# Spreading the last sixteen projection steps of two attention heads over their large query tiles

## The reference

```python
def block(args):
    qi, ci, s0 = args
    logits = jnp.einsum('bqhd,bkhd->bhqk', qi, k, preferred_element_type=jnp.float32) * scale
    logits = logits + (ci[..., :, None] - cum_k[:, :, None, :])
    qpos = s0 + jnp.arange(Q_BLOCK)
    mask = kpos[None, :] <= qpos[:, None]
    logits = jnp.where(mask[None, None], logits, -jnp.inf)
    p = jax.nn.softmax(logits, axis=-1)
    return jnp.einsum('bhqk,bkhd->bqhd', p.astype(v.dtype), v)
```

## Time and profile before

| | |
|---|---|
| median of 3 runs | 2994.4 us (2992.97 to 2999.1) |
| profiled execution, its time | 3002.76 us |
| its span | 3001.0 us |
| mean granted TensorE clock | 0.989 |
| PE busy | 2912.7 us, 97% of the span |
| DVE busy | 1492.5 us, 50% |
| ACT busy | 923.7 us, 31% |
| POOL busy | 1108.4 us, 37% |

### The profile page before, as it was taken

One profiled execution on the slowest core, in us unless ns is written; L12 is line 12 of the kernel. 1 busy time (PEld: TensorE's weight loads), 2 busy tenths in 40 slices (PEclk: granted clock), 3 DMA queues, 4 the chain that ended last, 5 costly groups with the idle time before them and its releaser, 6 DMA issues. The chain is left out here.

```text
span 3001.0 us, 37184 instructions
## 1 busy us (share of the span) xinstructions
PE 2912.7 (97%) x14772; PEld 2432.3 (81%) x14772; DVE 1492.5 (50%) x2202; ACT 923.7 (31%) x1628; POOL 1108.4 (37%) x585
## 2 busy tenths in 40 slices
PE   7999999999999999999999999999899999999997
PEld 3877778888888888888888887888788888888886
DVE  5842227887734413123134444545626666664645
ACT  5122226665113101011010111420325656563401
POOL 1332351111596434444343444334332332332341
PEclk9999999999999999999999999999899999999998
DMA  6534574331443111111111111111152222221111
GB/s 246 188 126 143 182 242 133 91 87 40 174 149 113 57 49 43 49 50 50 50 50 50 49 64 56 44 49 43 36 176 71 71 68 71 73 72 47 43 50 63
DMA packets 123821, 263.00 MB, mean 88 GB/s; under 512 B 48476, under 2 KB 74540, under 8 KB 119424
## 3 DMA queue, kind: packets, MB, share of 16 engines
q1 hardware_dynamic: 123648, 260.57, 26.2%
HBM read 215.97 MB, written 46.06 MB: 87 GB/s over the span
## 5 line engine op out<-in xcount | busy, mean ns | idle before, releaser
L881 POOL TENSOR_TENSOR whi<-raw,onesf 128x1024 fp32r<-128x1024 f32 x187 | 360.8, 1929 | 1293.1 <-PE ps L439 1188.1
L437 PE MATMUL ps<-Hb_hi,whi 128*128 128x512 f32 x1424 | 568.6, 399 | 10.3 <-DVE Y L2847 5.9
L439 PE MATMUL ps<-Hb_hi,wlo 128*128 128x512 f32 x1424 | 555.7, 390 | 0.0
L438 PE MATMUL ps<-Hb_lo,whi 128*128 128x512 f32 x1424 | 554.8, 390 | 0.0
L883 POOL TENSOR_TENSOR wlo<-raw,whi 128x1024 fp32r<-128x1024 f32 x187 | 500.2, 2675 | 14.7
L437 PEld LDWEIGHTS ps<-Hb_hi,whi 128*128 128x128 f32 x1424 | 267.7, 188 | 64.4 <-issue 8.5
L439 PEld LDWEIGHTS ps<-Hb_hi,wlo 128*128 128x128 f32 x1424 | 267.3, 188 | 57.1
L438 PEld LDWEIGHTS ps<-Hb_lo,whi 128*128 128x128 f32 x1424 | 268.1, 188 | 48.8
L1907 ACT ACTIVATE tmp<-ps 64x256 f32<-64x256 f32 (+3 forms) x112 | 61.7, 551 | 535.8 <-PE ps L439 465.3
L1907 ACT ACTIVATE tmp<-tmp,mx 128x1280 f32<-128x1280 f32 (+2 forms) x192 | 187.1, 974 | 80.7 <-DVE mx L3125 50.6
L437 PE MATMUL ps<-Uhi,whi 128*128 128x512 f32 x512 | 199.2, 389 | 0.0
(11 more groups left out here) (468 smaller groups left out, 5846.1 us busy)
## 6 DMA issues: line engine op xcount, KB each, us to landing
raw<-in_w SPq DMA_DIRECT2D x197, 512.0 KB, 3.5
adas<-in_ada SPq DMA_DIRECT2D x16, 1024.0 KB, 4.9
raw<-in_w SPq DMA_DIRECT2D x44, 256.0 KB, 3.8
adaE<-in_ada SPq DMA_DIRECT2D x4, 2048.0 KB, 23.0
gate_d<-gst SPq DMA_DIRECT2D x16, 512.0 KB, 2.8
v_d<-VS SPq DMA_DIRECT2D x2, 4096.0 KB, 14.2
ncB<-cum_d SPq DMA_DIRECT2D x16, 512.0 KB, 3.5
Vx<-v_d SPq DMA_DIRECT2D x16, 512.0 KB, 3.8
```

The lines of the kernel that those rows point to most:

```text
L437: nc.tensor.matmul(o, wh, xh, start=start, stop=False)
L438: nc.tensor.matmul(o, wh, xl, start=False, stop=False)
L439: return nc.tensor.matmul(o, wl, xh, start=False, stop=stop)
L881: nc.gpsimd.tensor_tensor(whi[b][:, 0:w], raw[b][:, 0:w], onesf[:, 0:1].to_broadcast([P, w]), ALU.mult).then_inc(S("split_hi"), 1)
```

## The change

Three things change, for heads 14 and 15 alone. The table `FILL_LAST` takes steps from rounds 2 to 5 and puts them into rounds 6, 7 and 8. ACT evicts the second half behind its last `flip_hi` of the head, not at tile 5. DVE evicts it behind its last `flip_lo` of the head, not at tiles 5 to 7.

```diff
 FILL = (4, 4, 4, 3, 2, 1, 2, 1, 2, 1)
-FILL_LAST = (3, 3, 3, 3, 2, 2, 0, 0, 0, 0)
+FILL_LAST = (3, 3, 2, 2, 1, 1, 1, 1, 2, 0)
...
# ACT's program
-                        if qt in (2, 5) and mine:
+                        if qt in (2, 5) and mine and not (qt == 5 and h >= FOX - 2):
                             project(*mine[qt // 4])
                     flip_hi(h, 7)
+                    if h >= FOX - 2:
+                        project(*mine[1])
                 other_half(FOX - 1, 3)
...
# DVE's program
                         if qt == 2 and mine:
                             project(*mine[0])
-                        if qt >= 5 and mine:
+                        if qt >= 5 and mine and h < FOX - 2:
                             kind, which, half = mine[1]
                             if kind == "kq":
                                 keys_queries(which, half, qt - 5)
...
                     for x in range(2):
                         flip_lo(h, 7, x)
+                    if h >= FOX - 2:
+                        project(*mine[1])
                 add(FOX - 1, 3)
```

## The result

| | before | changed |
|---|---|---|
| median, same comparison | 2997.16 us (12 runs, 2992.97 to 3002.98) | 3005.49 us (12 runs, 3001.99 to 3010.96) |
| profiled execution, its time | 3002.76 us | 3005.51 us |
| its span | 3001.0 us | 3003.7 us |

The changed kernel takes 1.0024 times as long, with an interval of 1.0015 to 1.0033: it is slower, by 8.3 us in the medians. The forecast was +5.2 us and 2999.6 us; the interval, 4.5 to 9.9 us, holds the difference, but the time lies outside the range of 2993.0 to 3003.5 us.

A forecast was written before the change was run, and what follows sets the result against it. PE sets the pace, with 4.82 us of pauses in heads 14 and 15. Rounds gave -2.27 us, 5.73 us more waiting at the border made +3.46, with the clock +5.2: 2999.6 us, range 2993.0 to 3003.5.

The forecast's parts named there:

- The likeliest case: Border of heads 14 and 15: late decay row, then 1.2 GHz for 2 to 5.4 us; +5.2 us, chance 0.47.
- the last line of the sum: Whole kernel: the +5.2 us put on a median of 2994.4 us, giving 2999.6 us, 0.17% more.
- part 3: Queue behind head 14's step 16: split, panel load and decay row slip; flips(15, 0) 4.48 us later, PE waits 6.5 us.
- Parts 1 and 2: Rounds of heads 14, 15: late waits removed, -2.56 and -1.50 us; thinner early rounds cost +0.83, +0.48, +0.48 us.
- 4.37 to the load: Chain behind step 16: SP issues the panel load 4.37 us after POOL begins splitting panel 25.
- The eviction ... lies wholly under this wait: Ahead of head 15's first tile: three ACT and three DVE instructions hidden under PE's 6.5 us wait for the row.
- rival A: Border of heads: decay row not held up, DVE's order decides; -0.9 us, 2993.5 us; chance 0.08.
- Part 4: Behind the pause at flips(15, 0): clock at 1.2 GHz for 3.6 us, 1.7 us lost, bounds 0 and 3.3.
- Rival B: Behind the pause: row late but clock stays at 2.4 GHz; +3.5 us, 2997.9 us; chance 0.12.
- rival C: Behind the pause: clock stays at 1.2 GHz for 7.0 us, 3.3 us lost; 6.8 us slower, 3001.2 us; chance 0.28.
- Rival D: Memory heads: keys and values late behind the split after head 15's step 16; about 1 us; chance 0.03.
- Rival E: Heads 14 and 15: every wait won, 4.82 us; 2989.6 us; chance 0.02.

The follow-up runs named there:

- e1: Changed kernel with head 15's decay row issued ahead of the panel load in SP's queue; stretch 67.80 us, ratio 1.0008 to the kernel before.
- e5: Kernel before, with its own table, but head 14's and 15's second half evicted behind the head's last flips; stretch 65.72 us, no ratio.
- e7: Changed kernel with 36 unused matmuls on PE ahead of flips(15, 0) to fill the pause; stretch 71.99 us, no ratio.
- e2: Changed kernel with only the table altered, so step 16 comes ahead of flips(14, 6); stretch 69.84 us, ratio 1.0007 to the kernel before.
- e10: As e6, with another table: three steps in round 2, two in round 4, none in round 5; stretch 63.88 us, ratio 0.9991 to before.
- e3: Changed kernel with 24 unused matmuls on PE ahead of flips(15, 0); stretch 73.22 us, ratio 1.0022 to the kernel before.
- e6: Changed kernel, decay row ahead of panel load, head 14's second half evicted behind head 15's first row_max and exps; stretch 63.51 us, 0.9986 to before.

## Why the prediction went wrong, point by point

**The likeliest case was the one that happened; the time was not in the range.** The forecast had the mechanism, its place and its sign, and a sum of +5.2 us. The three traces of the changed kernel give 5.5, 6.3 and 6.5 us more than before, the medians 8.3.

**The step that failed first** is the last line of the sum, "on it the change gives 2994.4 + 5.2 = 2999.6 us". The median of three runs that it stands on lay low: over the twelve runs of the comparison that tried the forecast it was 2997.16 us, in later comparisons on two chips 2998.78 and 3000.25 us, and single executions took 3000.23, 3001.13 and 3002.76. That is 2.8 us of the 5.9 that were missing, and it decides: with the base at 2997.16 the same range would have ended at 3006.3 us and held the 3005.49. Of the other 3.1 us the traces show 0.9 (6.1 us on average, where +5.2 was forecast), mostly in part 3 below; for 2.2 us they show nothing. The start of head 14 scatters by 7 us, which one trace can't show; the distance of 8.4 us between the profiled execution and the median was the hint. The clock has a part in this scatter, since its low stretches ahead of head 14 differ from trace to trace: by windows of 1 us PE worked at 0.50 for 34 us in the trace of before and for 26 us in e1, whose head 14 begins 7.0 us earlier. At 47% lost that is an estimated 4 of these 7 us.

**Parts 1 and 2, the rounds: right in the main.** The waits of the earlier trace rows went as forecast. `flips(14, 3)` waits 0.72 us (0.83 forecast), `flips(14, 4)` 0.81 (0.48), `flips(15, 4)` 0.57 (0.48), nothing at tile 5 and at `flips(15, 3)`. The rounds had 4.06 us of waits and have 2.10: -1.96 us, where -2.27 was forecast.

**Part 3, the queue: right in kind, mis-sized.** The term is "that is 5.73 us more of waiting". Measured, `flips(15, 0)` waits 7.30, 7.91 and 7.76 us and not 6.5, where it was 0.76: 6.5 to 7.2 us more. The main cause is the step "4.37 to the load": from POOL's start at 2694.45 to SP's load at 2699.56 it took 5.11 us, since the first half of the split ran into DVE's gate multiply and took 2.64 us, not 1.89. The other miss is the landing, 4.3 to 5.0 us in the changed kernel, inside the bounds of 3.5 and 5.0 that I gave, with 4.5 taken. A third, of 0.3 us, is POOL's start, half of it since I hung the chain on the start of `flips(14, 7)`, while POOL waits for the end of step 16's last matmul. The 0.38 us from load to row are exact. From `flips(14, 7)` to `flips(15, 0)` pass 11.05 us; 10.3 was forecast.

**"The eviction ... lies wholly under this wait": true, and it hid a second cause.** In the changed kernel the row is later than the CAST. Without the queue (e1) rival A's case comes about, for which I had -0.9 us; the stretch was 1.3 us longer than before. The forecast priced the eviction by two instructions, "0.68 + 0.69", which holds with POOL idle (e5), and took neither the CAST's collision with POOL's split (0.42 to 1.73 us) nor a fallen clock into account. The causes cover each other: mending the queue alone (e1) gave back 4.9 of 6.1 us and uncovered the rest. The reverse, the changed kernel with only the eviction moved, was not run.

**Part 4, the clock: right in kind, too dear.** 1.7 us forecast, 1.0 to 1.3 measured (rest 62.7 against 61.7 before and 61.4 in e7), since PE worked 3.0 us at 1.2 GHz and not 3.6. Rival B is out, rival C too: its 7.0 us are about what the low level lasted (6.8), but 3.9 us of them lay under the pause and cost nothing. The forecast counted the low level from the end of a pause only. e2, with 5.6 us of work at 1.2 GHz behind a shorter pause, shows what that leaves out.

**Rival D did not occur.** The fourth load for the memory heads went out at 2735.50 us, 4.8 us ahead of their first scores, and PE had no wait for them; the one wait there, 0.82 us for `Y`, is in both kernels. It was missing from the forecast's list, so "All this is 4.82 us, and no more can be won" does not hold: PE's waits in the stretch were 5.64 us. **Rival E** is out.

**What stays open.** The sum of the three terms agrees with the traces (-1.96 + 6.54 + 1.0 = 5.6, and 5.5 read off), but the medians differ by 8.3 and 7.0 us. Both intervals hold 5.5 to 6.5 us; whether the changed kernel loses more than the stretch shows in the executions without a trace stays open. One thing beyond it is shown: in e1, e2 and e10 the part behind the stretch took 264.2 to 264.5 us and not 263.4 to 263.5 as in the ten others, with no new wait of PE in it. In these three the clock fell some 240 us behind the stretch, near 2970 us, for some 3.4 us (e1: 0.74, 0.50 and 0.90 in the windows from 2970 to 2976 us); in the ten others it stayed at 1.00 over the same instructions. Such a fall costs 0.7 to 1.1 us, the difference in the part behind the stretch, and comes in some executions only. No trace of the changed kernel has this one, so it does not account for the distance.

## What to carry to other kernels

Before moving a step, ask what its last instruction releases, and follow that through every engine and each DMA queue up to the next thing that somebody waits for; here a step worth 0.69 us of cover carried a panel's release, and a small transfer that needed neither stood behind it in the queue. Issue a transfer with a near deadline ahead of one that only keeps a buffer full. When a chain slips by some microseconds, look up what it now runs beside, not only what it now runs behind; and put the range of a time of 3000 us on the scatter of more than three runs.

## What the runs showed of the hardware

**DVE and POOL hold each other up.** The CAST took 0.42 us in before, e2 and e5, and 1.73 to 1.76 us in the changed kernel's three traces, e1, e3 and e7, where it began 0.9 us into POOL's `wlo` (in e6 it began 0.15 us ahead of that one's end, and took 0.43); POOL's `whi` took 1.89 us alone and 2.64 us beside the gate multiply; that multiply took 1.21 us, and 2.18 (e2) and 2.62 us (e10) where the split had begun first; POOL's `wlo` 2.35 us, and 3.21 in e10. In each pair it is the one that starts later that grows, and the CAST ends 0.3 us after POOL's instruction, in e6 too. The Trainium skill, "SBUF — State Buffer", section "Who interferes with whom", has DVE and GpSimd share a pair of ports, of which whoever issues first holds it for its whole instruction while the other blocks; it names casts, and instructions with two inputs in SBUF against a GpSimd instruction that reads SBUF. The traces agree, and e10 shows it passed on: the multiply, begun 0.35 us behind `whi`, is held by it, and `wlo`, next in turn, is held by the multiply.

**The clock fell at pauses of under 3 us, and once in a while at none.** In e3 the granted clock went to 0.50 at 1.9 us into a pause of 2.43 us, in e1 at 1.4 us behind the end of one of 2.85 us, when PE was busy again; in e5, with a pause of 2.11 us, it stayed at 1.00. The rows at hand for the forecast were pauses of 4.48 and 7.76 us, and left that open. These are one trace each, and they are no threshold: the falls near 2970 us in e1, e2 and e10 came 0.5 to 1 us behind 16 short matmuls (128x1) with a single wait of 0.19 us among them, and ten other traces have the same instructions there and no fall.

**What a fall costs is not read off the pause.** The low level lasted 6.8 us in the changed kernel's three traces and in e2, and 3.4 us in e1 and e3. PE had work in 5.6 us of it in e2, whose rest of 64.0 us is the largest, and in 2.9 to 3.4 us in the others, whose rests are 62.7 to 62.9 us (61.4 in e7, without a fall).

**The row landed later behind a close neighbour.** The 512 KB of `ncB` take 3.5 us at the median; issued 0.38 us behind another 512 KB they took 4.3 to 5.5 us up to their first use in the changed kernel's traces, e2, e3 and e7. No run moved the neighbour away and left the rest as it was.
